# Pooling in a two-block transformer kernel: banded matmuls or shifted additions on GpSimd

## What is computed

```python
z = u @ w_in[l]
c_q, c_kv, k_rope, dq, dk, dv, p_in, z_gate = jnp.split(z, split_idx, axis=-1)
...
def pool_mixer(p, pool_w, pool_b, pool_scale):   # p: 256 tokens x 512 channels
    cs = jnp.cumsum(pf, axis=1)
    for g, w in enumerate((2, 4, 8, 16)):        # 128 channels to a window
        c = cs[..., sl]
        prev = jnp.pad(c, ((0, 0), (w, 0), (0, 0)))[:, :s]
        cnt = jnp.minimum(t + 1, w)
        outs.append((c - prev) / cnt - pf[..., sl])
    y = jnp.einsum('bsgc,gcd->bsgd', pooled, pool_w) + pool_b
    return y.reshape(b, s, POOL_WIDTH) * pool_scale
```

## Time and profile before

| quantity | value |
|---|---|
| three runs | 2051.55, 2051.63, 2051.82 us (median 2051.63) |
| the profiled execution, its own time | 2051.74 us |
| its span, first to last instruction | 2049.9 us |
| outside the span | 1.8 us |
| PE busy | 2039.5 us (99%) |
| DVE, ACT, POOL busy | 1385.7 (68%), 1018.4 (50%), 89.8 us (4%) |
| granted PE clock, mean | 0.999 |

### The profile page before, as it was taken

One profiled execution on the slowest core, in us unless ns is written; L12 is line 12 of the kernel. 1 busy time (PEld: TensorE's weight loads), 2 busy tenths in 40 slices (PEclk: granted clock), 3 DMA queues, 4 the chain that ended last, 5 costly groups with the idle time before them and its releaser, 6 DMA issues.

```text
span 2049.9 us, 25153 instructions
## 1 busy us (share of the span) xinstructions
PE 2039.5 (99%) x10364; PEld 1719.6 (84%) x10364; DVE 1385.7 (68%) x1626; ACT 1018.4 (50%) x1290; POOL 89.8 (4%) x131
## 2 busy tenths in 40 slices
PE   9999999999999999999999999999999999999998
PEld 7888888888888888888888888888888888888887
DVE  5655686775757566877575567657767667577675
ACT  6444576453444435675443465644444466444331
POOL 1001010000010001100100000000100000000000
PEclk9999999999999999999999999999999999999999
DMA  9655554465556556544656474555755645455552
GB/s 319 213 194 167 170 164 144 159 208 196 186 188 217 189 173 200 165 144 145 221 192 195 157 235 155 164 170 173 234 186 191 206 147 186 160 187 188 196 191 83
DMA packets 223729, 377.20 MB, mean 184 GB/s; under 512 B 6544, under 2 KB 109072, under 8 KB 223616
## 3 DMA queue, kind: packets, MB, share of 16 engines
q1 hardware_dynamic: 219792, 362.64, 53.7%
q0 software_dynamic: 3824, 12.97, 2.1%
HBM read 374.53 MB, written 1.05 MB: 183 GB/s over the span
## 4 chain that ended last, share of the span: by engine, by line
PE 96%; DVE 2%; ACT 1%; DMA 1%; issue 0%; POOL 0%; DVEq 0%; SPq 0%; ACTq 0%
PE pb L1613 64%; PE pb L1624 17%; PE pb L1627 9%; PE pb L1636 2%; DVE wl L2062 1%; PE pb L1682 1%; PE pb L1760 0%; DMA raw<-in_ffn_w_up_dram 0%; ACT wh L1850 0%; PE pb L1747 0%; PE pb L1824 0%; PE pb L1759 0%; DMA xg<-in_xg_dram 0%; PE pb L1739 0%; PE pb L1774 0%
## 5 line engine op out<-in xcount | busy, mean ns | idle before, releaser
L1850 ACT ACTIVATE wh<-raw 128x2048 fp32r<-128x2048 f32 (+4 forms) x351 | 658.3, 1876 | 627.2 <-PE pb L1613 250.5
L2062 DVE TENSOR_TENSOR wl<-raw,wh 128x2048 fp32r<-128x2048 f32 (+4 forms) x351 | 782.6, 2235 | 164.7 <-ACT wh L1850 164.3
L1613 PE MATMUL pb<-wh,x 128*128 128x512 f32 (+1 forms) x2224 | 676.3, 386 | 0.0
L1613 PEld LDWEIGHTS pb<-wh,x 128*128 128x128 f32 x2224 | 415.7, 188 | 80.9
L1613 PE MATMUL pb<-wl,x 128*128 128x512 f32 (+2 forms) x1112 | 439.0, 395 | 1.9 <-DVE wl L2062 1.8
L1624 PE MATMUL pb<-x,wh 128*128 128x512 f32 x1504 | 379.6, 394 | 0.0
L1624 PEld LDWEIGHTS pb<-x,wh 128*128 128x128 f32 x1504 | 271.6, 189 | 49.5
L1613 PE MATMUL pb<-wl,mh 128*128 128x512 f32 (+1 forms) x740 | 255.7, 391 | 0.0
L1613 PE MATMUL pb<-wh,ml 128*128 128x512 f32 (+1 forms) x740 | 253.7, 388 | 0.0
L1613 PE MATMUL pb<-wh,mh 128*128 128x512 f32 (+1 forms) x740 | 253.5, 388 | 0.0
L1613 PEld LDWEIGHTS pb<-wl,x 128*128 128x128 f32 x1112 | 209.0, 188 | 47.2 <-issue 3.7
(11 more groups left out here) (361 smaller groups left out, 1590.1 us busy)
## 6 DMA issues: line engine op xcount, KB each, us to landing
raw<-in_w_in_dram SPq DMA_DIRECT2D x100, 1024.0 KB, 5.3
raw<-in_w_ff_dram SPq DMA_DIRECT2D x64, 1024.0 KB, 5.3
raw<-in_ffn_w_down_dram SPq DMA_DIRECT2D x44, 1024.0 KB, 4.9
raw<-in_ffn_w_up_dram SPq DMA_DIRECT2D x43, 1024.0 KB, 5.3
raw<-in_ffn_w_gate_dram SPq DMA_DIRECT2D x42, 1024.0 KB, 5.3
raw<-in_w_branch_dram SPq DMA_DIRECT2D x24, 1024.0 KB, 5.0
raw<-in_w_out_dram SPq DMA_DIRECT2D x16, 1024.0 KB, 5.0
raw<-in_w_in_dram SPq DMA_DIRECT2D x4, 832.0 KB, 4.4
```

The source lines that it names most:

```text
L1613: ins = e.matmul(pb[b][:, 0:c1 - c0], x[:, s, cols], w[:, n, c0:c1], start=(it["first"] and n == 0 and q == 0), stop=(it["stop"] and n == ...
L1850: e.activation(hi, raw, ACT.Copy).then_inc(m.high_done, 1)
L2062: e.tensor_tensor(lo, raw, hi.bitcast(F32), ALU.subtract).then_inc(m.low_done, 1)
```

## The change

- `pin` leaves the first group; `dv` takes its place there. `pin` is now projected turned, by two wide groups of 256 columns right after `dkT` (where `dv` stood), with a new PE work `apart`: 24 matmuls of 256 columns for each 128 channels, all into one sum. ACT saves each of the four results (`pinsave`, 128 x 256) into `pp`, a buffer with 16 columns of zeros in front of each group's 256 tokens.
- `poolsum`, `poolcopy` and the load of `pc` are gone. A new work `windows` on POOL, next in the list after the last `pinsave`, adds shifted copies: four additions of 4 x 271, 3 x 269, 2 x 265 and 257 columns with `own_steps` between them, then four products of 16 columns that correct the first tokens. It stands ahead of `qrope` in POOL's queue.
- A new work `pooling` on DVE, placed in `latent_kv` behind `ksave`, waits for the sums and makes mean less token (four instructions of 128 x 256).
- `pool()` enters lane 3 only after `latent_kv`, so `poolmix`, `poolbias` and `poolsplit` run in the gates: after one more yield, the first at the third tick, the second at the fourth.
- `weigh` and `wcopy` of the differential pairs no longer wait for the pooling.

```diff
-        self.group(self.cols(W, l, 0, 0, c_epi, 416) + self.cols(W, l, 1952, 1, self.copy_t("pin", pin)), start=True)
+        self.group(self.cols(W, l, 0, 0, c_epi, 416) + self.cols(W, l, 1440, 1, self.copy_t("dv", self.dv)), start=True)
...
         def pool():
-            yield
             yield
             for i in range(2):
                 use = self.side()
-                v = self.pe("poolsum", i=i, use=use, need=list(pin), l=l)
-                self.add("poolcopy", i=i, use=use, p=v["p"])
-                got = use
-                yield
-            self.pin_free = [v["p"]]
-            for i in range(2):
-                use = self.side()
-                v = self.pe("poolmix", i=i, use=use, need=[("evac", got)], l=l)
+                v = self.pe("poolmix", i=i, use=use, need=[("pooled", l + 1)], l=l)
                 self.add("poolbias", i=i, use=use, p=v["p"], l=l)
                 yield
             self.add("poolsplit", use=use, n=l)
...
-        self.group(self.cols(W, l, 1440, 0, self.copy_t("dv", self.dv)))
-        while not pool_done or ("C", 2, 1) not in self.ready or ("C", 2, 0) not in self.ready:
+        for q in range(2):
+            def pin_epi(i, p, use, q=q):
+                self.add("pinsave", g=2 * q + i, p=p, use=use)
+                pin.append(("evac", use))
+            self.wide_group((W, (l,), 0, 8, 1952 + 256 * q, 256), self.pair(q), pin_epi, "apart")
+        self.add("windows", need=list(pin))
+        while ("C", 2, 1) not in self.ready or ("C", 2, 0) not in self.ready:
             self.pump()
         self.add("krrope", n=l, need=[self.ready["C", 2, 0], self.ready["C", 2, 1]])
...
-        self.latent_kv(l, q_toks)
+        self.latent_kv(l, q_toks, lambda: self.add("pooling", n=l))
+        self.lanes[3].append(pool())
...
             self.add("ksave", i=i, p=pk[i], use=uses[i])
+        then()
         self.add("qrope", n=l, need=q_toks, p=pk[1])
...
+        elif k == "windows":
+            pp, sa, sb, end = m.pp, m.sa, m.sb, 16 + S
+            po.all_ready(it["need"])
+            po.step(e.memset(pp[:, :, 0:16], 0.0))
+            po.own_steps()
+            po.step(e.tensor_tensor(sa[:, :, 1:end], pp[:, :, 1:end], pp[:, :, 0:end - 1], ALU.add))
+            po.own_steps()
+            po.step(e.tensor_tensor(sb[:, :, 3:end], sa[:, 1:4, 3:end], sa[:, 1:4, 1:end - 2], ALU.add))
+            po.own_steps()
+            po.step(e.tensor_tensor(sa[:, 2:4, 7:end], sb[:, 1:3, 7:end], sb[:, 1:3, 3:end - 4], ALU.add))
+            po.own_steps()
+            po.step(e.tensor_tensor(sb[:, 2, 15:end], sa[:, 3, 15:end], sa[:, 3, 7:end - 8], ALU.add))
+            po.own_steps()
+            po.wait_ge(m.short_landed, 16)
+            sums = m.window_sums()
+            for g in range(4):
+                ins = e.tensor_tensor(sums[g][:, 0:16], sums[g][:, 0:16], m.short[:, g, :], ALU.mult)
+            ins.then_inc(m.summed, 1)
...
+        elif k == "apart":
+            hi, lo = m.weights(it["j"])
+            bank, c = pb[use[0]], slice(i * P, i * P + P)
+            pe.wait_ge(m.low_done, it["j"] + 1)
+            pe.all_ready(it["need"])
+            pe.wait_ge(m.evac[use[0]], use[1])
+            for s in range(8):
+                e.matmul(bank[:, 0:S], hi[:, s, c], m.xh[:, s, :], start=(s == 0), stop=False)
+                e.matmul(bank[:, 0:S], hi[:, s, c], m.xl[:, s, :], start=False, stop=False)
+                ins = e.matmul(bank[:, 0:S], lo[:, s, c], m.xh[:, s, :], start=False, stop=(s == 7))
+            ins.then_inc(m.pe_done, 1)
...
+        elif k == "pinsave":
             a.pe(p)
-            e.activation(m.pair_of(("pT", i)), bank[:, :], ACT.Copy).then_inc(m.evac[use[0]], 1)
+            e.activation(m.pT[:, it["g"], :], bank[:, 0:S], ACT.Copy).then_inc(m.evac[use[0]], 1)
...
+        elif k == "pooling":
+            v.wait_ge(m.summed, n + 1)
+            for g, x in enumerate(m.window_sums()):
+                ins = e.scalar_tensor_tensor(m.pT[:, g, :], x, 0.5 ** (g + 1), m.pT[:, g, :], ALU.mult,
+                                             ALU.subtract)
+            ins.then_inc(m.pooled, 1)
```

More of the change, by code:

```diff
@@ L45, in constants @@
     freq = np.broadcast_to(np.stack([f1, f1, f2, f2]).reshape(1, 64), (P, 64))
[L46 to L54, removed]
+    short = np.array([[w / min(t + 1, w) for t in range(16)] for w in (2, 4, 8, 16)], np.float32)
     s = q[:, None]
@@ L61, in constants @@
         "c_ident": ident, "c_mask": mask, "c_freq": np.ascontiguousarray(freq),
-        "c_pool": np.ascontiguousarray(np.concatenate([p0, p1], 1)),
+        "c_short": short,
         "c_tril": np.concatenate([tril, chunk], 1),
@@ L179, in sbuf @@
         self.bn = A("bn", take(128), [P, 2, 16])
+        self.short = A("short", take(256), [P, 4, 16])
         self.epsc = A("epsc", take(32), [P, 8])
@@ L333, in half, with window_sums @@
         return self.cols[name][:, 2 * q + i, :]
+    def window_sums(self):
+        return [x[:, g, 16:16 + S] for x, g in ((self.sa, 0), (self.sb, 0), (self.sa, 2), (self.sb, 2))]
     def row(self, name, t):
@@ L545, in group, with wide_group @@
             self.tick()
-    def wide_group(self, key, banks, epi):
+    def wide_group(self, key, banks, epi, work="wide"):
         j = self.take(key)
@@ L556, in wide_group @@
             use = self.use(banks[i])
-            v = self.pe("wide", j=j, i=i, use=use, need=need)
+            v = self.pe(work, j=j, i=i, use=use, need=need)
             epi(i, v["p"], use)
@@ L974, in diff_pair @@
             yield
-        while not self.pin_free or len(self.dv) < 2:
+        while len(self.dv) < 2:
             yield
@@ L1053, in mixer1 @@
         diff_done, mla_done = [], []
-        pin, self.dv, self.pin_free = [], [], []
+        pin, self.dv = [], []
         self.clear("C", range(3))
@@ L1182, in merged_ready, with latent_kv @@
             self.m_free[s] = self.np - 1
-    def latent_kv(self, l, q_toks):
+    def latent_kv(self, l, q_toks, then):
         j = self.take(("mla_w_ukv", (l,), 0, 1, 0, 1024))
@@ L1532, in pool_program @@
             e.dma_start(m.scan[:, :], m.A["c_scan"]).then_inc(m.const_landed, 16)
+            e.dma_start(m.short[:, :, :], m.A["c_short"].partition_broadcast(P)).then_inc(m.short_landed, 16)
             e.memset(m.ones[:, :], 1.0 / P)
@@ L1642, in pe_program @@
                                stop=True)
-            ins.then_inc(m.pe_done, 1)
-        elif k == "poolsum":
-            bank = pb[use[0]]
-            pe.all_ready(it["need"])
-            pe.wait_ge(m.pc_landed, 16 * (l + 1))
-            pe.wait_ge(m.evac[use[0]], use[1])
-            for g in (2 * i, 2 * i + 1):
-                o, gs = (g % 2) * S, slice(g * P, g * P + P)
-                e.matmul(bank[:, o:o + 256], m.pin[:, 0, gs], m.pc[:, 256 * g:256 * g + 256], start=True, stop=False,
-                         skip_group_check=True)
-                ins = e.matmul(bank[:, o + 128:o + 256], m.pin[:, 1, gs], m.pc[:, 1024 + P * g:1024 + P * g + P],
-                               start=False, stop=True, skip_group_check=True)
             ins.then_inc(m.pe_done, 1)
@@ L1910, in act_program @@
             e.activation(m.row(it["dst"], t), bank[:, :], ACT.Copy).then_inc(m.evac[use[0]], 1)
-        elif k == "poolsum":
-            pass
-        elif k == "poolcopy":
+        elif k == "pinsave":
             a.pe(p)
-            e.activation(m.pair_of(("pT", i)), bank[:, :], ACT.Copy).then_inc(m.evac[use[0]], 1)
+            e.activation(m.pT[:, it["g"], :], bank[:, 0:S], ACT.Copy).then_inc(m.evac[use[0]], 1)
         elif k == "poolsplit":
             a.emptied(use)
-            e.activation(m.yph[:, :, :].rearrange("p a s -> p (a s)"), m.pT[:, :, :].rearrange("p a s -> p (a s)"),
-                         ACT.Copy).then_inc(m.pool_high, 1)
+            e.activation(m.yph[:, :, :], m.pT[:, :, :], ACT.Copy).then_inc(m.pool_high, 1)
         elif k == "qsave":
@@ L2225, in dve_program @@
         elif k == "poolsplit":
-            pT, hi, lo = [w[:, :, :].rearrange("p a s -> p (a s)") for w in (m.pT, m.yph, m.ypl)]
             v.wait_ge(m.pool_high, n + 1)
-            e.tensor_tensor(lo, pT, hi.bitcast(F32), ALU.subtract).then_inc(m.pool_low, 1)
+            e.tensor_tensor(m.ypl[:, :, :], m.pT[:, :, :], m.yph[:, :, :].bitcast(F32), ALU.subtract).then_inc(m.pool_low, 1)
         elif k == "krrope":
```

21 lines of the change are left out of this document (9 added, 12 removed).

## The result

The changed kernel takes **2064.76 us** (median of six runs, 2064.11 to 2066.37) where the kernel before took 2051.67 in the same session: ratio 1.0065, 95% interval 1.0055 to 1.0075. It is slower by 13.1 us, 6.55 per layer. The forecast was 2061.9, slower, by VectorE held while `kr` is turned. That happened, but the sum had +10.3 us, 2.8 less than the 13.1 measured.

The account below looks back on a forecast made before the run. PE, busy 99%, was taken to bound the kernel. Per layer -1.97 - 0.20 + 5.45 + 1.0 + 0.85 = +5.13 us, +10.3 for two, gave 2061.9 us; range 2047.0 to 2066.0.

Parts of the forecast that it names:

- first wait: PE before the second `weigh` in mixer 1, because POOL's additions delay DVE up to the end of `krrope`: +5.45 us per layer.
- clock: PE's granted clock falls to half after the new wait of 5 us: 0 to 1.7 us, taken as +0.85 per layer.
- second wait: PE waits for the second pair's `combine`, behind `pooling` and `qrope` meeting: 0 to 2.3 us, taken as +1.0 per layer.
- third wait: PE before the third pair's `dscore`, for `wcopy` on ACT to empty its bank; the prediction had no term for it.
- `poolsum` gone: Both `poolsum` leave PE between the dk halves, loss of switching float formats included: -2.61 us per layer.
- `pin` turned: On PE, `pin` becomes 96 matmuls of 256 columns instead of 48 of 512, at 0.12 us each: +0.64 us per layer.
- old wait gone: PE's wait before a `weigh` for ACT's `pcopy` in mixer 1 goes: -0.20 us per layer.
- DVE is held.: POOL's additions hold DVE's two-operand `low` and `krrope` ahead of `weigh`; three additions taken, 5.7 us; chance 0.55.
- The first rival: DVE keeps its way: POOL waits for DVE, never the reverse; 2047.3 us, up to 2049 with some wait; chance 0.30.
- One of the signs that it gave: A `low` or a step of `krrope` would start late with DVE idle before it; no size given.
- alone it costs nothing: `pooling`'s four DVE instructions behind `ksave`, 1.9 us, ahead of the second pair's `combine`, against 1.8 us of slack.
- Ahead of nothing that PE needs before the `weigh` works.: `poolbias` and `poolsplit` come behind the second pair's `combine` and delay nothing PE needs before the `weigh` works; no price.

Follow-up runs that it names:

- e4: Changed kernel with 18 matmuls of 512 columns, result overwritten, put on PE into the wait before the first pair's second `weigh`; 2060.50 us.
- e3: Kernel before the change with four POOL additions and four products of 16 columns put between the `dv` group and `krrope`, writing a spare buffer; 2065.51 us.
- e1: Changed kernel without POOL's four additions and four short products, the means left out; 2051.82 us.
- e2: Changed kernel with POOL's additions and products replaced by memsets of the same buffers, about as long in all; 2051.95 us.
- e8: e6 with both `poolmix` at one visit of the lanes and `poolsplit` at the next; 2047.12 us.
- e9: Changed kernel with each of POOL's four additions made twice in a row; 2067.98 us.
- e10: e1 with DVE's `pooling` of means also left out, except one instruction of 16 columns; 2047.07 us.
- e5: Changed kernel with POOL's window sums waiting for the end of `krrope`; 2056.16 us.
- e6: Changed kernel with the edits of e5 and e7 together; 2070.90 us.
- e7: Changed kernel with `pooling` moved from behind `ksave` to lane 3, after the second pair's `dscore` and `combine`, and `poolmix` two ticks later; 2083.86 us.

## Why the prediction was right, and where it was off

It came out as forecast, slower and inside the range, by the mechanism that it named. That the sum came within 2.9 us has some luck in it: the first wait was put 1.0 us too high per layer, while the clock was put 1.4 too low, the second wait 0.4 too low, and the third was not there at all. And the range was wide enough to take in the rival's 2047.3. Step by step, per layer (measured in layer 0 by differences of start times against the kernel before; the waits of 0.20 and 4.48 are the idle times of the list):

| step | predicted | measured |
|---|---|---|
| group ahead of `dqT`, `pin` and `dv` exchanged | 0 | 0.0 |
| `poolsum` gone | -2.61 | -2.64 |
| `pin` turned | +0.64 | +0.52 |
| old wait gone | -0.20 | -0.20 |
| first wait | +5.45 | +4.48 |
| `mla_w_uq` group, faster | 0 | -0.23 |
| clock | +0.85 | +2.24; 2.1 by e4 |
| second wait | +1.0 | +1.39 (idle 1.19) |
| third wait | 0 | +1.10 (idle 0.97) |
| sum | +5.13 | +6.7; 6.55 by the medians |

- **PE's work.** Right within 0.2 us, in both terms. `apart` ran at 0.12 us a step, as `lowrank` did in the earlier trace rows. With the group for `mla_w_uq`, which no term had, PE's work came out at -2.35, 0.38 us below the sum's -1.97.
- **"DVE is held."** Right, and shown: e3 makes the wait out of the additions alone, e1 and e2 take it away. The first rival, DVE keeps its way, is refuted by the `low` pair of 6.29 us and the step of 1.52. One of the signs that it gave was wrong: no `low` and no step starts late with DVE idle before it, the delay is in their durations. And the start times do not say who goes first: in the earlier trace rows `qrope`'s third step starts at 267.36, the `low` 0.45 us later, and yet the `low` keeps its 2.28 us and POOL waits. In e8 an addition (263.21, 3.42 us) and a `low` (263.74, 2.28) meet in the same way. What decides a first meeting, no run shows.
- **The size of the first wait.** +5.45 was 1.0 too much. The prediction took three additions at 2.5, 1.9 and 1.3 us; with nothing in the way they took 2.10, 1.53 (e9) and 1.07, 1.9 to 2.0 ns a column in all, where it had reckoned 2.1 and a fixed 0.21 on top. Each hold was shorter still (1.80, 1.34, 0.83). It counted one turn too few: four additions held DVE, the fourth for 0.48. In all the hold was 4.45 where the sum had 5.7. Against that, PE did not come 0.45 us later to `weigh` (3 x (2.88 - 2.72) is 0.48, a slip of 0.03): the group for `mla_w_uq` was 0.23 shorter. So there was no slack of 0.25, and the wait is the hold, 4.48 and 4.45. The errors partly cancel. That further additions can slip in only at `krrope`'s own waits was the right picture, which e9 confirms with 6.20 us.
- **The clock.** This is the term that was mis-sized most: 0.85 taken, 2.1 to 2.2 measured, above even its upper end of 1.7. That end came from the earlier trace rows, the sixteen matmuls at the start of one execution. The same sixteen in the profile of the changed kernel:

```profile
0.98 6.75 PE L1664 MATMUL pb<-fill 128*128 128x512 f32 x16 [0.98 <-POOL fill L1518]
```

By the prediction's own working that is 6.75 - 3.8 = 2.9 us, so one start was no upper end. In mixer 1 the clock was low from about 259.7 to 266.5 (worked out from the windows above), and PE was at work for 4.8 us of that.
- **Behind `ksave`.** 1.0 taken, 1.19 of idle time measured and 1.39 by start times. (PE's printed durations overlap the next start: a pair of 512 columns prints 0.62 us and costs 0.455, so an idle time is short by about 0.16. That is also why the third wait is 1.10 and not 0.97.) The named mechanism fits. `pooling` took 0.70, 0.95, 0.95 and 0.96 us beside `qrope`, where each takes 0.42 with POOL idle (e8). The second of the four:

```profile
270.56 0.95 DVE L2228 SCALAR_TENSOR_TENSOR pp<-sb,pp 128x256 f32<-128x256 f32 x1
```

  From the first of them to the `low` behind them it is 3.26 us, in e8 1.35 (276.33 to 277.68). The 1.9 us between are more than the wait, so "alone it costs nothing" fits too. It is an estimate from rows: e1 has the same wait, but meets `qrope` as well (3.33 us), e10 takes `pooling` away whole, and no run has it in this place with POOL idle.
- **"Ahead of nothing that PE needs before the `weigh` works."** This failed. After the `weigh` works comes a `dscore`, which needs banks that `wcopy` empties. On ACT `poolsplit` (`yph`, 1.05 us) stands directly ahead of `wcopy`, and on DVE the two `poolbias` pairs (2 us) and `pooling` stand ahead of the weights that `wcopy` follows. The third wait, 1.1 us, was in no term. (That `pooling` is needed for it is shown by e10; the part of `poolbias` and `poolsplit` is read from the order of the queues.)
- **The costs of one layer** then read 2.5 saved, and 4.5 + 2.2 + 1.4 + 1.1 paid. The second and third wait alone cancel the saving (e1: no change at all); the first and its clock are the 13 us.

Three of my own expectations failed, e5 by 4.7 us, e6 and e7 by more than 23, all by the same slip: I asked who waits for the moved step, and not behind what it now stands. The next run was laid out from that question, and it gave 2047.12 where 2047.3 was expected.

What stays open: which of DVE and POOL goes first when they meet; how much of the third wait is `poolbias` and how much `poolsplit`; and why layer 1 costs 0.3 us more than layer 0 in the profiled pair.

## What to carry to other kernels

Before work is moved to GpSimd, look for what VectorE does in that stretch with two operands in SBUF: each such instruction, however short, can cost nearly a whole GpSimd instruction (1.80 us of 2.10), so a chain of short dependent steps on the critical path pays once per step. And when a step is moved in a list that is also every engine's queue, follow it to both sides, who waits for it and what it now stands ahead of and behind on each engine, to the next thing that TensorE asks for: here one visit of the lanes made 2047.1 us out of 2070.9.

## What the runs showed of the hardware

- **Two engines taking turns.** With both queues full of instructions that read two SBUF operands, neither starves: each gets one instruction at a time, and the hold lies inside the recorded duration (0.18 us became 1.98, with no idle time before it). `ksave`, a copy out of PSUM, is no such instruction: in e8 the additions beside it kept their 1.53 and 1.08 us, and it its 2.81.
- **A fall of the clock in the middle of a kernel** cost 2.1 us beside a wait of 4.5, and 18 matmuls of no use in that wait bought it back. It is cheaper than what the wait itself costs, but it made this wait half as dear again. The waits of 1.2 and 1.0 us in the gates left the clock at 1.00 (from 280 to 284 and from 294 to 298).
